# Attention kernel: maxima turned in one matmul, masks of the first pass on VectorE, openings in parts between products

## The reference

```python
for blk in range(T // Q_BLOCK):
    lo, hi = blk * Q_BLOCK, (blk + 1) * Q_BLOCK
    s = jnp.einsum('bqhd,bkhd->bhqk', q[:, lo:hi], k[:, :hi]) * scale
    if log_decay_cum is not None:
        s = s + (cum[:, :, lo:hi, None] - cum[:, :, None, :hi])
    mask = (lo + jnp.arange(Q_BLOCK))[:, None] >= jnp.arange(hi)[None, :]
    p = jax.nn.softmax(jnp.where(mask, s, -jnp.inf), axis=-1)
    outs.append(jnp.einsum('bhqk,bkhd->bqhd', p, v[:, :hi]))
```

## Time and profile before

| | us |
|---|---|
| median of three runs | 2560.76 |
| the profiled execution's own time | 2564.89 |
| its span | 2563.1 |
| TensorE busy | 2378.3 (93%) |
| VectorE busy | 1163.1 (45%) |
| ScalarE busy | 917.1 (36%) |
| GpSimd busy | 792.6 (31%) |

### The profile page before, as it was taken

The page is one execution under the profiler, slowest core; times in us unless marked ns, Lnnn a source line. Parts: engine busy times, 40 slices in busy tenths (PEclk is TensorE's granted clock), DMA queues, the critical chain, the costliest instruction groups (busy, mean ns, idle before and its releaser), DMA issues.

```text
span 2563.1 us, 35660 instructions
## 1 busy us (share of the span) xinstructions
PE 2378.3 (93%) x14804; PEld 1818.5 (71%) x14804; DVE 1163.1 (45%) x1756; ACT 917.1 (36%) x1508; POOL 792.6 (31%) x740
## 2 busy tenths in 40 slices
PE   7988999898999999899999889989999999998998
PEld 7867877885695876555696778778756858765556
DVE  4278144624335226565423872255342451266542
ACT  4332225513334333344332322263143243334341
POOL 1264211212514520354413532211134144203452
PEclk9989999999999999999998999999999999999999
DMA  4100331230100213100311003403201002131003
GB/s 145 53 18 2 93 121 38 99 115 1 34 17 1 64 38 115 58 1 1 133 67 53 18 1 99 148 6 133 81 1 34 17 1 64 37 115 58 1 1 123
DMA packets 91873, 141.33 MB, mean 55 GB/s; under 512 B 18208, under 2 KB 65344, under 8 KB 91712
## 3 DMA queue, kind: packets, MB, share of 16 engines
q1 hardware_dynamic: 91712, 139.05, 15.8%
HBM read 105.48 MB, written 33.55 MB: 54 GB/s over the span
## 4 chain that ended last, share of the span: by engine, by line
PE 77%; DVE 15%; ACT 3%; issue 2%; POOL 1%; DMA 1%; SPq 0%; POOLq 0%; DVEq 0%; ACTq 0%
PE psum L237 32%; PE psum L491 12%; PE psum L1379 6%; PE psum L1364 4%; PE psum L1333 4%; DVE gla_A L750 3%; PE psum L1365 3%; PE psum L1367 3%; PE psum L1346 2%; PE psum L1318 2%; PE psum L729 2%; PE psum L1386 1%; PE psum L981 1%; PE psum L1766 1%; DVE mla_nm L1514 1%
## 5 line engine op out<-in xcount | busy, mean ns | idle before, releaser
L196 POOL TENSOR_TENSOR w_lo<-w_raw,w_hi 128x2048 fp32r<-128x2048 f32 (+3 forms) x60 | 274.8, 4581 | 1013.0 <-ACT w_hi L189 1013.0
L237 PE MATMUL psum<-w_hi,h_hi 128*128 128x256 f32 (+3 forms) x1280 | 188.8, 291 | 20.7 <-ACT fox_k L1153 15.7
L237 PE MATMUL psum<-h_hi,w_hi 128*128 128x512 f32 x768 | 204.5, 410 | 0.0
L237 PE MATMUL psum<-h_lo,w_hi 128*128 128x512 f32 x768 | 198.8, 402 | 0.0
L1577 POOL TENSOR_TENSOR mla_acc<-mla_acc,mla_p 128x512 f32<-128x512 f32 (+3 forms) x160 | 164.5, 1043 | 109.6 <-ACT mla_p L1447 108.5
L237 PE MATMUL psum<-h_hi,w_lo 128*128 128x512 f32 x768 | 192.0, 392 | 0.0
L237 PEld LDWEIGHTS psum<-w_hi,h_hi 128*128 128x128 f32 x1280 | 169.5, 196 | 28.1 <-ACT fox_k L1153 16.5
L237 PE MATMUL psum<-w_lo,h_hi 128*128 128x256 f32 (+3 forms) x1280 | 180.8, 284 | 3.4 <-POOL w_lo L196 3.4
L237 PE MATMUL psum<-w_hi,h_lo 128*128 128x256 f32 (+3 forms) x1280 | 183.9, 288 | 0.0
L189 ACT ACTIVATE w_hi<-w_raw 128x2048 fp32r<-128x2048 f32 (+3 forms) x60 | 113.4, 1894 | 187.9 <-PE psum L491 172.8
L1577 POOL TENSOR_TENSOR fox_acc<-fox_acc,fox_p 128x512 f32<-128x512 f32 (+3 forms) x160 | 149.0, 950 | 91.0 <-ACT fox_p L1447 90.2
(11 more groups left out here) (318 smaller groups left out, 4504.4 us busy)
## 6 DMA issues: line engine op xcount, KB each, us to landing
w_raw<-in_w_in_dram SPq DMA_DIRECT2D x38, 1024.0 KB, 5.3
out_dram<-x_rows SPq DMA_DIRECT2D x64, 512.0 KB, 2.6
x_rows<-out_dram SPq DMA_DIRECT2D x56, 512.0 KB, 5.2
w_raw<-in_w_out_dram SPq DMA_DIRECT2D x16, 1024.0 KB, 6.6
x_first<-in_x_dram SPq DMA_DIRECT2D x8, 512.0 KB, 7.8
x_rows<-in_x_dram SPq DMA_DIRECT2D x8, 512.0 KB, 5.8
w_raw<-in_w_in_dram SPq DMA_DIRECT2D x2, 1088.0 KB, 9.1
w_raw<-in_w_in_dram SPq DMA_DIRECT2D x2, 1056.0 KB, 7.9
```

The source lines that it names most:

```text
L196: pool.tensor_tensor(self.w_lo[c["set"]][:, :n], self.w_raw[c["set"]][:, :n], self.w_hi[c["set"]][:, :n].bitcast(F32), ALU.subtract).then_ ...
L237: last = pe.matmul(o, lhs, rhs, start=(kk == 0 and n == 0), stop=(kk == KT - 1 and n == 2))
```

## The change

In the first pass the mask matmul is gone. `maximum` on VectorE now handles a diagonal tile in two instructions: a reduction of the columns left of the diagonal block, and a `tensor_tensor_reduce` that adds the mask to the 128 diagonal columns in PSUM and writes the minimum of the negated sums. One further reduction joins up to three candidates per query tile, for every item.

`turn_max` turns all four query tiles' maxima in one float32 matmul, into rows of their own (and for fox a row of ones ahead of them, for row 64). `place_max` moves to VectorE and spreads the four rows over four rows of the query tile, each times a 0/1 pattern (`max_rows`, a new constant and one more DMA at the start), so that each row is non-zero for its own 128 queries. The key tile has ones in these rows. The fox tiles no longer need zeros up to row 96.

The openings are written out anew. The four units around which they stand are split into their products (for outB into its parts), and turns, scores and turned maxima stand between these; the unit results use PSUM banks 0 and 1 (4, 5, 0 and 1 for outB) while banks 2 and 3 take the scores. ScalarE's and VectorE's programs follow the same order.

Besides: fk0's rounding moves before the last three evacuations of fq, fv0's behind the first of fk; outB's two chunks exchange their weight sets, and their roundings move between the evacuations of the latent queries; outC0's rounding and split move into the third attention, at (1, 8) and (2, 6).

```diff
-M_ROW = 96
-NEG = -1e30
+NEG, KEEP = -1e30, 3e38
...
     def score_pe(self, pe, i, n):
-        diagonal = hi == (qt + 1) * P
-        last = pe.matmul(out, q[:M_ROW, a, x * P:(x + 1) * P], kk[:M_ROW, a, :hi - lo], start=True, stop=not diagonal)
-        if diagonal:
-            last = pe.matmul(out[:, hi - lo - P:], k.ident_bf[:, :], k.mask_bf[:, :], start=False, stop=True)
-        last.then_inc(self.scores.sem, 1)
+        pe.matmul(out, q[:D, a, x * P:(x + 1) * P], kk[:D, a, :hi - lo], start=True, stop=True).then_inc(self.scores.sem, 1)
 
     def turn_max(self, pe, i, a):
-        for x in range(4):
-            last = pe.matmul(k.psum[M_ROW:M_ROW + 1, self.misc_bank("m", i, a), x * P:(x + 1) * P],
-                             self.nmax[:, i, a, x:x + 1], k.ident[:, :], start=True, stop=True)
-        last.then_inc(self.m_turned.sem, 1)
+        pe.wait_ge(self.max_joined.sem, self.max_joined.at(2 * i + a + 1))
+        pe.matmul(k.psum[self.M:self.R, self.misc_bank("m", i, a), :P], self.nmax[:, i, a, :], k.ident[:, :], start=True,
+                  stop=True).then_inc(self.m_turned.sem, 1)
...
     def maximum(self, dve, i, n):
-        dve.tensor_reduce(out, self.k.psum[:, 2 + u % 2, :hi - lo], AX_X, ALU.max, negate=True).then_inc(self.max_done.sem, 1)
+        if part < c:
+            dve.tensor_reduce(nm[:, 0:1], ps, AX_X, ALU.max, negate=True).then_inc(self.max_done.sem, 1)
+            return
+        if w > P:
+            dve.tensor_reduce(nm[:, 1:2], ps[:, :w - P], AX_X, ALU.max, negate=True)
+        dve.tensor_tensor_reduce(ps[:, w - P:w], ps[:, w - P:w], k.mask_bf[:, :], -1.0, KEEP, ALU.add, ALU.min,
+                                 nm[:, 2:3]).then_inc(self.max_done.sem, 1)
+        if x == 3:
             dve.wait_ge(self.max_done.sem, self.max_done.at(u + 1))
+            dve.tensor_reduce(self.nmax[:, i, a, self.width - self.M:], self.nm[:, c, a, :, :], AX_X, ALU.min)\
                .then_inc(self.max_joined.sem, 1)
+
+    def place_max(self, dve, i, a):
+        p, c = self.items[i]
+        r, n = slice(self.M, self.R), self.R - self.M
+        dve.wait_ge(self.m_turned.sem, self.m_turned.at(2 * i + a + 1))
+        dve.tensor_tensor(self.q_hi[(2 * p + c) % self.QS][r, a, :].rearrange("r (x q) -> r x q", x=HH),
+                          self.k.psum[r, self.misc_bank("m", i, a), :P].unsqueeze(1).to_broadcast([n, HH, P]),
+                          self.k.max_rows[r, :].unsqueeze(2).to_broadcast([n, HH, P]), ALU.mult)\
+           .then_inc(self.m_done.sem, 1)
...
     def vector(self, dve, hook=None):
                 for n in self.scores_at(i, j):
                     self.maximum(dve, i + 1, n)
+                if self.m_at(i, j) is not None:
+                    self.place_max(dve, i + 1, self.m_at(i, j))
                 if i and j == 4:
                     self.refine(dve, i - 1)
...
+def open_fox(pe, att, unit, product, banks_free):
+    unit(pe, 0)
+    att.turn(pe, 0, 0)
+    att.turn(pe, 0, 1)
+    unit(pe, 1)
+    att.turn(pe, 0, 2)
+    att.turn(pe, 0, 3)
+    product(pe, 2, 0)
+    banks_free(pe)
+    att.score_pe(pe, 0, 0)
+    att.score_pe(pe, 0, 1)
+    product(pe, 2, 1)
+    att.score_pe(pe, 0, 2)
+    att.score_pe(pe, 0, 3)
+    product(pe, 2, 2)
+    att.score_pe(pe, 0, 4)
+    att.score_pe(pe, 0, 5)
+    att.turn(pe, 0, 4)
+    product(pe, 3, 0)
+    att.score_pe(pe, 0, 6)
+    att.score_pe(pe, 0, 7)
+    att.turn(pe, 0, 5)
+    product(pe, 3, 1)
+    att.turn_max(pe, 0, 0)
+    att.turn(pe, 0, 6)
+    product(pe, 3, 2)
+    att.turn_max(pe, 0, 1)
+    att.turn(pe, 0, 7)
...
+def open_vector(dve, att, adds=None):
+    att.rest_of_group(dve, 0, 0)
+    att.rest_of_group(dve, 0, 1)
+    if adds is not None:
+        adds(dve, 0)
+    att.rest_of_group(dve, 0, 2)
+    att.rest_of_group(dve, 0, 3)
+    if adds is not None:
+        adds(dve, 1)
+    for n in range(6):
+        att.maximum(dve, 0, n)
+    if adds is not None:
+        adds(dve, 2)
+    att.rest_of_group(dve, 0, 4)
+    att.maximum(dve, 0, 6)
+    att.maximum(dve, 0, 7)
+    att.rest_of_group(dve, 0, 5)
+    att.place_max(dve, 0, 0)
+    if adds is not None:
+        adds(dve, 3)
+    att.rest_of_group(dve, 0, 6)
+    att.place_max(dve, 0, 1)
+    att.rest_of_group(dve, 0, 7)
...
-    for t in range(1, TT):
+    for t in range(1, 5):
         half.evac(act, "fq", t)
     k.round_chunk(act, L, "fk0")
-    k.round_chunk(act, L, "fv0")
+    for t in range(5, TT):
+        half.evac(act, "fq", t)
```

More of the change, by code:

```diff
@@ L312, in plan_layer @@
     gate("gB1", 1, 1, 1)
+    k.ring, k.turn = (0, 1), 0
     gate("gB0", 1, 0, 0)
+    k.ring, k.turn = (2, 3, 0, 1), 0
     chunk("fq0", "T", C_BQ, HALF_W, 0)
     chunk("fk0", "T", C_BK, HALF_W, 1)
-    chunk("fv0", "T", C_BV, HALF_W, 0)
+    k.add_chunk(layer, "fv0", "T", C_BV, HALF_W, 0)
+    for t in range(TT):
+        if t == 4:
+            k.ring, k.turn = (0, 1), 0
+        k.add_unit(layer, "fv0", t, "act")
+    k.ring, k.turn = (2, 3, 0, 1), 0
     chunk("lat1", "T", C_CQ, Q_RANK, 0)
@@ L322, in plan_layer @@
     expand(1)
-    out("outB", 1, 0)
+    out("outB", 1, 1)
     out("outC", 2, 0)
@@ L1236, in misc_uses @@
     def misc_uses(self):
-        yield from (("pre", 0, g) for g in range(8))
-        yield from (("m", 0, a) for a in range(2))
+        yield from (("m", 0, g) if what == "m" else ("pre", 0, g) for what, g in self.opening)
         for i in range(self.NI):
@@ L1364, in scores_turned @@
         pe.matmul(out, self.k_hi[ks][:R, a, keys], self.q_hi[qs][:R, a, lo:], start=True, stop=False)
-        pe.matmul(out, self.k_hi[ks][:M_ROW, a, keys], self.q_lo[qs][:M_ROW, a, lo:], start=False, stop=False)
+        pe.matmul(out, self.k_hi[ks][:D, a, keys], self.q_lo[qs][:D, a, lo:], start=False, stop=False)
         diagonal = kb >= 4 * c
-        last = pe.matmul(out, self.k_lo[ks][:M_ROW, a, keys], self.q_hi[qs][:M_ROW, a, lo:], start=False, stop=not diagonal)
+        last = pe.matmul(out, self.k_lo[ks][:D, a, keys], self.q_hi[qs][:D, a, lo:], start=False, stop=not diagonal)
         if diagonal:
@@ L1388, in row_sums @@
         last.then_inc(self.rs_done.sem, 1)
-    def begin_pe(self, pe, groups=()):
-        for n in range(8):
-            self.score_pe(pe, 0, n)
-            if n % 2 and groups:
-                self.turn(pe, 0, groups[n // 2])
-        for a in range(2):
-            self.turn_max(pe, 0, a)
     def tensor(self, pe):
@@ L1538, in out @@
         dve.tensor_tensor(at, self.k.psum[:, 4 + i % 2, :], at, ALU.mult).then_inc(self.y_done.sem, 1)
-    def begin_dve(self, dve, groups=()):
-        for n in range(8):
-            self.maximum(dve, 0, n)
-            if n % 2 and groups:
-                self.rest_of_group(dve, 0, groups[n // 2])
     def vector(self, dve, hook=None):
@@ L2108, in tensor_mla @@
     a.outB.group(pe, 1, 0)
-    a.outB.group(pe, 1, 1, behind=lambda pe, x: a.attC.turn(pe, 0, x))
+    out, att = a.outB, a.attC
+    for i in range(3):
+        out.wait_part(pe, i, 1, 1)
+    for x in range(2):
+        for i in range(3):
+            out.part(pe, i, 1, 1, x)
+        att.turn(pe, 0, 2 * x)
+        att.turn(pe, 0, 2 * x + 1)
+    out.part(pe, 0, 1, 1, 2)
+    out.part(pe, 1, 1, 1, 2)
+    k.evacuated(pe, L, "outB0", TT - 1)
+    att.score_pe(pe, 0, 0)
+    att.score_pe(pe, 0, 1)
+    out.part(pe, 2, 1, 1, 2)
+    att.score_pe(pe, 0, 2)
+    att.score_pe(pe, 0, 3)
+    out.part(pe, 0, 1, 1, 3)
+    att.score_pe(pe, 0, 4)
+    att.score_pe(pe, 0, 5)
+    att.turn(pe, 0, 4)
+    out.part(pe, 1, 1, 1, 3)
+    att.score_pe(pe, 0, 6)
+    att.score_pe(pe, 0, 7)
+    att.turn(pe, 0, 5)
+    out.part(pe, 2, 1, 1, 3)
+    att.turn_max(pe, 0, 0)
+    att.turn(pe, 0, 6)
+    att.turn_max(pe, 0, 1)
+    att.turn(pe, 0, 7)
     k.evacuated(pe, L, "outB1", TT - 1)
-    a.attC.begin_pe(pe, (4, 5, 6, 7))
-    a.attC.tensor(pe)
+    att.tensor(pe)
 def scalar_program(act, k, setup, layers):
@@ L2543, in vector_mla @@
     mla1.mean_dve(dve, link, 3)
[L2544 to L2545 removed]
+    a.attC.blank_rows(dve, 0)
     a.outB.add(dve, 1, 0)
[L2547 to L2551 removed]
+    a.attC.blank_rows(dve, 1)
+    open_vector(dve, a.attC, lambda dve, x: a.outB.add_one(dve, 4 + x, 1))
+    a.attC.blank_rows(dve, 2)
     def between(dve, i, j):
```

192 lines of the change are left out of this document (91 added, 101 removed).

## The result

The changed kernel takes 2637.5 us (median of four runs, 2634.1 to 2647.7) where the kernel before, on the same chip, takes 2561.4: a ratio of 1.030, 95% interval 1.028 to 1.031. 2472 was forecast, 2440 to 2506 as the range. The profiled execution took 2636.8, its span is 2635.0.

What follows compares the result with a forecast made beforehand. TensorE, busy 93% of the span with 77% of the chain, was taken as the bound. Openings 46, fk0 10 and items 33.6, less 1.5 of small costs, gave 88 us off: 2472 us, range 2440 to 2506.

Steps and rivals of the forecast that it cites:

- the items' part: Attention items: fewer mask and maxima products on TensorE, less VectorE's added work, gain 16.8 us a layer, 33.6 in both.
- Rival A: Items over four key blocks: slow clock returns once in each of 16, at 1.6 us; 2497 us, chance 0.13.
- fk0: First unit of fk0: earlier rounding and split remove TensorE's waits and the slow clock behind them, 5 us a layer.
- Openings: Starts of a layer's three attentions: shortened to 28.2, 20.0 and 21.9 us, together a gain of 23.0 a layer.
- the stalls I allowed: TensorE's waits left in the openings: second, 1.6, 0.3 and 0.8 us; third, 2.9, 0.8 and 1.3.
- Masks and maxima: Attention items, TensorE's side: masks save 1.0 to 1.3 us an item, turned maxima 1.45; VectorE's longer maxima take some back.
- The latent item 1: Latent attention: the second unit waits for the placing behind the key scaling, 1.05 us later than now, a loss.
- x: VectorE's masked reduction: extra time for writing its result column, taken as 0.10 us, with ends 0 and 0.2.
- Rival D: VectorE: masked reduction far dearer than its width, paces items and openings; slower, 2581 us at 1.2 us extra; chance 0.04.
- Small ones: Extra DMA ahead of the positions costs 0.5 us, weight roundings between latent query evacuations 1; together 1.5 lost.
- outC0's split: Moved with its rounding into the third attention: costs nothing, or 2 us if that cover fails.
- The sum: Whole kernel: gains of 46, 10 and 33.6 us less 1.5 make 88, giving 2472 us from the median.

Runs made afterwards that it cites:

- b_k65: The kernel before with only its fox score and correcting products cut from 96 rows to 65; 2639.6 us, ratio 1.030.
- a_pad96: The changed kernel with its fox contractions filled back up to 96 rows with zeros, by added memsets; 2544.0 us, ratio 0.994.
- a_hooks: a_pad96 with its memsets moved, and VectorE's scalings for the later latent pairs moved away from the placings; 2525.3 us, ratio 0.986.
- after_twice: The changed kernel (65 rows) with each first-pass score product issued twice in items over four key blocks and in openings; 2659.2 us, ratio 1.038.
- a_open2: The kernel before with only the change's openings, fk0 rounding and order of weight sets, memsets moved out of the way; 2530.1 us, ratio 0.989.
- a_pad_fill: a_pad96 with sixteen useless products where TensorE stands still around the latent attention's first item; 2536.3 us, ratio 0.992.
- b_items: The kernel before with only the change's masks, maxima, turns and placing on VectorE, over 96 rows, old openings; 2622.9 us, ratio 1.024.
- b_items_turn4: b_items with each turned-maxima product issued four times into the same place; 2596.2 us, ratio 1.013.
- b_items_fill: b_items with 18 useless products in each opening; 2598.8 us, ratio 1.016.
- b_turn1: b_items with the first pass's masks back on TensorE; 2617.2 us, ratio 1.022.
- a_act: a_pad96 with its memsets moved and ScalarE placing the latent maxima, except in the opening; 2536.1 us, ratio 0.990.
- after_full: The changed kernel (65 rows) with useless 128-row identity products ahead of the scores in items over four key blocks and openings; 2555.2 us, ratio 0.997.

## Why the prediction was wrong

**The step that failed** is the items' part, 16.8 us a layer, and within it an edit that stands nowhere in my sum: the fox products over 65 and 69 rows instead of 96 and 97. Taken alone it costs 80 us (b_k65); taken out of the change it gives back 93 (a_pad96), with 268 us less at half clock in the fox items. I had read that a product's duration goes by its columns, and left out that the clock may go by its rows. No row of the kernel before could have priced it, but it was an unshown operation and should have had bounds like the masked reduction.

**Rival A** (the clock falls in c=0 items) was the right mechanism at the wrong price. I took 1.6 us a fall, from fk0, where wide products follow; in the first two c=0 items of every attention a fall lasts 14 to 24 us, 6 to 9 us are lost in it (22.2 for 15.5, 25.9 for 17.2), and 4 to 6 in the c=1 item behind. Sixteen items at 25 us in all became up to 176. What I held against it, 1.00 in the first item, held for an item of 96 rows with its maxima in eight products, and both were being removed. The Trainium skill, "TensorE: Matmul & The Clock Gate" (HAM oscillation), names repeated stalls as what brings the slow clock back. The runs agree for part of the latent attention: falls of 13.7 us hold its waits of 4.06 us (1126.06) and 8.16 us (1154.44) in the changed kernel, and in a_hooks, where the first of these waits is gone, item 2 goes from 24.7 to 17.2 us. In the fox items something else decides: b_k65 falls with the instructions of the kernel before and no wait over 0.65 us in items 0 and 2, and after_twice stays low while TensorE hardly waits.

**Openings**, 23.0 a layer: right as lengths, 14.5, 3.5 and 9.4 come out (27.4). But that is not what reaches the end: in a_open2 two latent items behind them take 19.8 and 37.3 us for 16.9 and 31.7. Of the stalls I allowed, the second shows 0.61 and 0.29, the third 0.72 and 1.09.

**fk0**, 5 a layer: right. From 725 to 759 each group of eight starts 0.96 behind the last, with no wait, and from fq's first group to the opening it is 5.3 us less than before.

**Masks and maxima at full clock.** Read from items that ran at 1.00: a later c=0 item goes from 18.5 to 17.2 (1.3; forecast 1.05 to 1.5), a c=1 item from 27.3 to 25.4 (1.9; forecast 2.45), the first item of the second fox attention from 16.8 to 15.6 in a_pad96 (1.2; forecast 2.0). An attention's last item, for which nothing was forecast, goes from 19.2 to 19.9. A whole fox attention gains 4.0 at full clock, not 5.5. The latent item 1 loses 2.8, not 1.05 (30.1 in a_pad_fill, 3.4 of them at half clock): its second unit waits for the placing behind the key scaling, as foretold, but for 3.10 us there. The score's wait of the earlier trace rows is now:

```profile
597.53 0.56 PE L1351 MATMUL psum<-fox_k_hi,fox_q_hi 65*128 65x512 f32 x2
598.91 0.50 PE L1351 MATMUL psum<-fox_k_hi,fox_q_hi 65*128 65x512 f32 x1 [0.82 <-DVE fox_nm L1501]
```

0.82 for 0.47. Turned maxima, of the earlier trace rows: `x64` products of 336 ns for `x256` of 289.

**x, the masked reduction's second half.** The reductions, and the accumulator reads of the fox ones, with ns min/median/max:

```profile
L1505 DVE CUSTOM_DVE_ANT_0 psum<-psum,mask_bf x256: 281/289/300, 583.7 to 2556.9; 128x128 f32<-128x128 f32 x128
L1505 DVE DVE_READ_ACCUMULATOR2_ANT fox_nm<- x128: 132/140/143, 583.9 to 2164.6; 128x1 f32 x128
```

0.28 for the reduction, as taken. That it would come as two instructions is what the Trainium skill, "VectorE: DVE Perf Modes" (Two Vector instructions with no wait between them), says; the trace agrees. But the read begins 0.21 behind the reduction's start, and a next reduction that waits for nothing begins with it (1021.06, 1021.26, 1021.26 in a_pad96), as a plain reduction over 128 columns lets its next one begin after 0.20. Only the 64 joins, which wait for the read, begin 0.37 to 0.38 behind: 0.17 for every head and item. So x is 0 for most of them and under 0.05 on average, not 0.10. Rival D is out.

**Small ones.** One that I put at nothing, and 2 if its cover fails, is not small: outC0's split, moved to GpSimd at (2, 6) of the latent attention. There VectorE's first rotation product runs beside it. Before and after, and then TensorE's wait in the changed kernel:

```profile
1117.25 0.86 DVE L1618 TENSOR_TENSOR mla_rope_tmp<-mla_q,cos 128x512 f32<-128x512 f32 x1
...
1145.31 4.51 POOL L196 TENSOR_TENSOR w_lo<-w_raw,w_hi 128x2048 fp32r<-128x2048 f32 x1
1145.88 4.49 DVE L1616 TENSOR_TENSOR mla_rope_tmp<-mla_q,cos 128x512 f32<-128x512 f32 x1
...
1154.44 1.06 PE L1337 MATMUL psum<-ident,mla_q 128*96 128x128 f32 x4 [8.16 <-DVE mla_q L1621]
```

The product lasts 4.49 us for 0.86, TensorE's wait for the rotation grows from 2.71 to 8.16, and the latent item 3 from 31.7 to 36.5 us a layer, where I had forecast a gain. It goes with the split and not with the items: in a_open2, with the items of before, the product lasts 4.92 and the item 37.3, and in b_items, with the split where it was, 0.68 and 31.2. No kernel moves the split alone, so this is as far as it is shown. The other small ones can't be told apart from the clock.

**The sum.** At full clock it is 2461 against 2472 forecast; that figure charges half of every us at the lower clock, also where TensorE waited, so it is a lower bound. That the two come so near is in part luck: the openings gave more than forecast, the fox items and outC0's split less.

**What stays open.** It is not known why the items' part at 96 rows, behind the openings of before, keeps an attention's first item at half clock: products added at the seam cure it wholly or partly (b_items_turn4, b_items_fill), and so do the new openings (a_pad96); masks don't (b_turn1). What decides was not found, nor why latent items, which have 96 rows, fall where they hardly wait (a_hooks at 1133.1). It was not tried either whether the fall in fox items comes at 80 rows or only at 65.

## What to carry to other kernels

Ask of every edit to a TensorE-bound stretch what it does to the granted clock, and price a fall by the stretch it will last for, not by the shortest one in the trace. Dropping unused rows of a contraction is not free: rows of zeros held the clock at 2.4 GHz here, and were worth 80 us. An engine that fills in for another (placing on VectorE) takes on the waits of its new queue, and such a wait can cost more than its length: where the 3.11 and the 4.07 us were taken away, the items got 4.5 and 7.5 us shorter (a_act, a_hooks). And work moved under a quiet engine can still slow its neighbour (outC0's split).

## What the runs showed of the hardware

- The granted clock depends on how many rows TensorE's products take, not only on how busy it is: 26.7 of 27.9 us busy over 65 and 97 rows at 0.56, 16.5 of 18.5 over 96 and 97 rows at 1.00 (item 2 of b_k65 and of the kernel before), with zeros in the rows that make the difference.
- Useless products can pay: 128-row ones gained 82 us (after_full); 65-row ones cost 22 (after_twice).
- An item entered at half clock can stay there to its end: 24.2 us in five of the six attentions of b_items, where at full clock it is over in 15.5. The c=1 item behind is back at 1.00 after some 4 us.
- VectorE and GpSimd can hold each other up: one product of the rotation, 0.68 to 0.95 us elsewhere, took 4.5 to 5.0 in all fourteen kernels in which GpSimd's split of outC0 (4.5 to 5.1 us) ran beside it.
